# Two conditioning loads requested at another place, and the latents' copies put ahead of a split

## What is computed

```python
def modulated(x, g, mod, s):
    h = rmsnorm(x, g)
    return h * (1 + mod[:, s, 1][:, None]) + mod[:, s, 0][:, None]

for i in range(DEPTH):
    mod = silu(c) @ w_ada[i] + b_ada[i]             # 9 vectors of 1024 for each sequence
    x = x + 0.5 * g0 * swiglu(modulated(x, 0))
    x = x + g1 * (short_conv if i == 0 else mla)(modulated(x, 1))
    x = x + 0.5 * g2 * swiglu(modulated(x, 2))

# short_conv:  b, c, v = split(h @ w_in);  y = (b * conv(c * v)) @ w_out
# mla:         d = h @ w_in;  cq, ckv, kr = rmsnorm(d[:384]), rmsnorm(d[384:640]), rope(d[640:])
#              q = cq @ w_uq;  attention over ckv, kr and a paged cache;  @ w_o
```

## Time and profile before

| | us |
|---|---|
| median of 3 runs | 1253.67 |
| lowest and highest run | 1250.36, 1256.72 |
| the profiled execution | 1254.01 |
| its span | 1252.0 |

### The profile page before, as it was taken

How to read it: one execution, slowest core, us unless ns; L and a number is a source line. 1 busy time by engine, 2 the same in 40 slices (tenths; PEclk the granted TensorE clock), 3 DMA queues, 4 the chain that set the end, 5 groups by cost and what they waited for, 6 DMA issues and landing times.

```text
span 1252.0 us, 23786 instructions
## 1 busy us (share of the span) xinstructions
PE 1220.3 (97%) x9968; PEld 1142.7 (91%) x9968; DVE 674.0 (54%) x1021; ACT 523.9 (42%) x724; POOL 152.8 (12%) x144
## 2 busy tenths in 40 slices
PE   6999999999999999999999999998999999999997
PEld 5999999989999999999899999987776689999997
DVE  5545445466675444455544545456855466554453
ACT  4434343343335534433543433355633345454332
POOL 0000002300040000023000001210445040000031
PEclk9999999999999999999999999999999999999998
DMA  9877655468766774355677444575577563444442
GB/s 359 333 285 291 220 204 183 171 207 295 269 234 235 289 290 165 132 177 185 245 280 279 184 139 159 187 267 195 194 259 265 183 234 135 169 168 158 140 164 82
DMA packets 70617, 269.47 MB, mean 215 GB/s; under 512 B 5408, under 2 KB 5920, under 8 KB 56704
## 3 DMA queue, kind: packets, MB, share of 16 engines
q1 hardware_dynamic: 33888, 184.57, 40.5%
q10 hardware_dynamic: 29792, 59.09, 12.9%
q0 software_dynamic: 6848, 24.52, 5.9%
HBM read 266.55 MB, written 1.62 MB: 214 GB/s over the span
## 4 chain that ended last, share of the span: by engine, by line
PE 90%; DVE 4%; DMA 3%; ACT 2%; ACTq 1%; issue 1%; DVEq 0%; SPq 0%
PE bank L1473 24%; PE bank L1475 24%; PE bank L1474 24%; PE bank L1518 4%; PE bank L1858 3%; PE bank L1920 1%; PE bank L1872 1%; DVE w_lo L940 1%; ACT w_hi L677 1%; PE bank L1539 1%; ACTq L689 1%; PE bank L1540 1%; PE bank L1532 1%; PE bank L1646 1%; DMA stage<-in_w_uq 1%; DMA stage<-in_w_ci 1%
## 5 line engine op out<-in xcount | busy, mean ns | idle before, releaser
L940 DVE TENSOR_TENSOR w_lo<-stage,w_hi 128x2048 fp32r<-128x2048 f32 (+2 forms) x178 | 365.9, 2057 | 295.9 <-ACT w_hi L677 295.3
L1473 PE MATMUL bank<-h_hi,w_hi 128*128 128x288 f32 (+1 forms) x1576 | 467.8, 297 | 2.1 <-DVE w_lo L940 1.2
L1475 PE MATMUL bank<-h_hi,w_lo 128*128 128x288 f32 (+1 forms) x1576 | 465.0, 295 | 0.0
L1474 PE MATMUL bank<-h_lo,w_hi 128*128 128x288 f32 (+1 forms) x1576 | 464.4, 295 | 0.0
L677 ACT CAST w_hi<-stage 128x2048 fp32r<-128x2048 f32 (+2 forms) x178 | 296.7, 1669 | 251.4 <-PE bank L1475 175.6
L1473 PEld LDWEIGHTS bank<-h_hi,w_hi 128*128 128x128 f32 (+1 forms) x1576 | 295.5, 187 | 6.9 <-issue 3.3
L1475 PEld LDWEIGHTS bank<-h_hi,w_lo 128*128 128x128 f32 (+1 forms) x1576 | 295.5, 187 | 0.0
L1474 PEld LDWEIGHTS bank<-h_lo,w_hi 128*128 128x128 f32 (+1 forms) x1576 | 295.4, 187 | 0.0
L1475 PE MATMUL bank<-gu_hi,w_lo 128*128 128x288 f32 x768 | 227.6, 296 | 0.0
L1473 PE MATMUL bank<-gu_hi,w_hi 128*128 128x288 f32 x768 | 227.0, 296 | 0.0
L1474 PE MATMUL bank<-gu_lo,w_hi 128*128 128x288 f32 x768 | 224.0, 292 | 0.0
(11 more groups left out here) (263 smaller groups left out, 1049.7 us busy)
## 6 DMA issues: line engine op xcount, KB each, us to landing
stage<-in_w_gu SPq DMA_DIRECT2D x85, 1024.0 KB, 4.9
stage_ada<-in_w_ada ACTq DMA_DIRECT2D x53, 1024.0 KB, 9.3
stage<-in_w_down SPq DMA_DIRECT2D x64, 704.0 KB, 4.0
stage<-in_w_ci SPq DMA_DIRECT2D x16, 768.0 KB, 4.3
stage_ada<-in_w_ada SPq DMA_DIRECT2D x9, 1024.0 KB, 14.6
ada_early<-in_w_ada SPq DMA_DIRECT2D x4, 1024.0 KB, 16.6
stage<-in_w_co SPq DMA_DIRECT2D x4, 1024.0 KB, 6.9
stage<-in_w_wo SPq DMA_DIRECT2D x4, 1024.0 KB, 5.0
```

The costliest lines, as they stand in the source:

```text
L940: nc.vector.tensor_tensor(w_lo[part][:, 0:cols], stage[st_][:, 0:cols], w_hi[part][:, 0:cols], ALU.subtract).then_inc(lo_ready, 1)
L1473: nc.tensor.matmul(out, hi, x_hi, start=start, stop=False)
L1474: nc.tensor.matmul(out, hi, x_lo, start=False, stop=False)
L1475: return nc.tensor.matmul(out, lo, x_hi, start=False, stop=stop)
```

## The change

In the convolution's input product the four quarters of the second group are issued one in each of the four next steps with a unit (6 to 9), behind that step's split (`run`; `after` is told by `spaced` not to issue them). The latents' group is no longer issued by ScalarE: SyncE issues it ahead of its request of query unit 1, behind a wait for the last residual ahead of norm 4 (`x_ready`) and for the products of the group before (`ada_used`). In the last step of `mla_in` ScalarE copies the unit's tiles first and splits query unit 1 afterwards; in the two steps before the order stays.

```diff
--- before.py
+++ after.py
@@ -545,6 +545,11 @@
                 for st in steps(sp, seg, peel_first=seg.base == 0) if seg.n else ():
                     if st.u is None or isinstance(st.u, int) and st.u < OPEN_UNITS:
                         continue
+                    if st.kind == "uq" and st.place == 1:
+                        sp.wait_ge(x_ready, KT * MLA_BLOCK)
+                        sp.wait_ge(ada_used, LATENT + OPEN_MORE)
+                        for q in range(RING):
+                            sp.dma_start(by_run(ring_latent[q]), quarter(LATENT, q)).then_inc(ada_loaded[q], 16)
                     if isinstance(st.u, int) and st.u == OPEN_UNITS + 1:
                         sp.wait_ge(lo_ready, 1)
                     elif not isinstance(st.u, int) or st.u > OPEN_UNITS:
@@ -683,10 +688,10 @@
 
             SPACED = between_step(act, 1)
 
-            def load_ada(j, into=ring):
+            def load_ada(j):
 
                 for q in range(RING):
-                    act.dma_start(by_run(into[q]), quarter(j, q)).then_inc(ada_loaded[q], 16)
+                    act.dma_start(by_run(ring[q]), quarter(j, q)).then_inc(ada_loaded[q], 16)
 
             def root(n):
                 act.wait_ge(stats_ready, n + 1)
@@ -717,19 +722,18 @@
                     nc.scalar.activation(h_hi[:, kt, 0:TP], h_fp[:, kt, 0:TP], ACT.Identity,
                                          bias=mods[:, 3 * KT * n + kt, 0:1]).then_inc(h_hi_ready, 1)
                 if n == 1:
-                    after(SPACED)
+                    after(SPACED, spaced=True)
                 elif n and between_step(act, n):
                     after(between_step(act, n))
 
-            def after(st):
+            def after(st, spaced=False):
                 if st.kind == "ada":
                     act.wait_ge(ada_used, st.place + OPEN_MORE + 1)
                     act.wait_ge(asum_done, st.place + OPEN_MORE)
                     of = SUM_BANK.get(st.place, 6) if isinstance(st.place, int) else 6
                     nc.scalar.copy(ada_tok[:], bank[of][:, 0:2 * P]).then_inc(tok_copied, 1)
-                    if st is not SPACED and (not isinstance(st.place, int) or st.place < LATENT):
-                        load_ada(st.place + 1, ring_latent if isinstance(st.place, int) and st.place + 1 == LATENT
-                                 else ring)
+                    if not spaced and (not isinstance(st.place, int) or st.place + 1 < LATENT):
+                        load_ada(st.place + 1)
                 if st.kind == "gu":
                     m, n_m = st.tile, FT * st.unit.block + st.tile
                     act.wait_ge(unit_used, st.u + 1)
@@ -746,12 +750,16 @@
                     nc.scalar.copy(one(gu_hi, st.tile), conv_acc[:]).then_inc(y_hi_ready, 1)
 
             def run(name):
+                group, q = SPACED.place + 1, 0
                 for st in steps(act, SEG[name], split=True, peel_first=name == "ffn0_gu"):
                     split_ahead(st)
-                    if name == "conv_in" and st.u is not None and st.u - SEG[name].base in range(RING):
-                        q = st.u - SEG[name].base
-                        act.dma_start(by_run(ring[q]), quarter(SPACED.place + 1, q)).then_inc(ada_loaded[q], 16)
-                    after(st)
+                    if name == "conv_in" and st.u is not None and q < RING:
+                        act.dma_start(by_run(ring[q]), quarter(group, q)).then_inc(ada_loaded[q], 16)
+                        q += 1
+                    again = name == "conv_in" and st.kind == "ada" and st.place == SPACED.place + 1
+                    after(st, spaced=again)
+                    if again:
+                        group, q = st.place + 1, 0
 
             def open_h_hi(kt):
                 act.wait_ge(normed, kt + 1)
@@ -810,7 +818,9 @@
 
             norm(MLA_BLOCK)
             for st in steps(act, SEG["mla_in"], split=True):
-                split_ahead(st)
+                last = 2 * st.place + 2 > QT + RT
+                if not last:
+                    split_ahead(st)
                 act.wait_ge(unit_used, st.u + 1)
                 for b, t in zip(st.banks, range(st.tile, st.tile + 2)):
                     if t < QT + RT:
@@ -819,6 +829,9 @@
                     else:
                         nc.scalar.copy(kr_raw[0:ROPE], bank[b][0:ROPE, 0:T])
                         nc.scalar.copy(kr_raw[ROPE:P], bank[b][0:ROPE, 0:T]).then_inc(d_ready, 1)
+                if last:
+                    split_ahead(st)
+
             def latent_root(i, n, dst):
                 act.wait_ge(lat_stats, i + 1)
                 nc.scalar.activation(dst[:], bank[6 + i][:, 0:T], ACT.Sqrt, bias=eps[:, 0:1], scale=1.0 / n)\
```

## The result

| | before | after |
|---|---|---|
| median of the runs side by side (20 each), us | 1253.93 | 1256.57 |
| lowest and highest run, us | 1250.36, 1256.72 | 1254.32, 1259.36 |
| the profiled execution, its span, us | 1254.01, 1252.0 | 1256.49, 1254.9 |
| mean granted clock of the profiled execution | 0.997 | 0.993 |

The ratio is 1.0017, 95% interval 1.001 to 1.0024: **slower**, by about 2 us by the ratio and 2.6 by the medians, where 1.8 us faster was forecast. That is within 0.5%, but outside the range of 1249.0 to 1256.0.

A forecast was written before the change was run, and what follows sets the result against it. The prediction took TensorE as the bound, with only its gaps to win, 4.55 us or 0.36%. From 1254.01 us it took off 0.71 (convolution) and 1.09 (attention), giving 1252.2, range 1249.0 to 1256.0.

The forecast's parts named there:

- What bounds the kernel: Whole kernel: TensorE busy 1220.3 of 1252.0 us, so only its gaps can be won; the four total 4.55 us, 0.36%.
- The convolution: Convolution's input product: pacing the second group's quarters removes TensorE's gap; bounds 0 to 0.71 us gain, 0.71 taken.
- The latents' issues: Attention's input product: without ScalarE's issues unit 2 is split earlier, its 0.57 us gap goes, query unit 1 requested 4.0 us earlier.
- The landing: Attention: when query unit 1's load arrives behind the latents, between 848.0 and 850.3, against 849.97 today; 848.0 taken.
- The near end: Attention: query unit 1 lands at 848.0, by 7.37 MB at 384 GB/s; a gain of 1.09 us, taken.
- the far end: Attention: query unit 1 lands at 850.3, by 7.37 MB at 337 GB/s; a loss of 0.31 us.
- rival (a): Attention: latents ahead in the same ring delay query unit 1 to 848.7 to 851.7; 1253.5 us, chance 0.15.
- signs of being wrong: Query unit 1's cast waits for DMA and query product's gap exceeds 4 us; or units 12 and 13's casts stop TensorE.
- The reorder: Attention's last input step, copies before split: 1.52 us gap moves to the query product's start, nearly 3 us remaining there.
- (b): Attention: same ring lands query unit 1 from 850.7 on, losing more than the convolution wins; 1255.0 us, chance 0.11.
- (c): Convolution: its gap stays or moves because paced quarters delay units 12 and 13; 1252.9 us, chance 0.10.
- (d): Attention: unit 2's cast waited for something other than the issues, so the 0.57 us stay; 1252.8 us, chance 0.07.

The follow-up runs named there:

- experiment 1: Only the convolution's second group issued in four parts, against the kernel before; 1255.04 us, ratio 1.0002.
- experiment 8: Kernel before plus the convolution's part, latents still from ScalarE but two quarters behind the split in each of the first two input steps; 1253.67 us, ratio 0.9994.
- 9: Changed kernel without the reorder, query unit 1 requested by ScalarE instead of SyncE, latents early on SyncE; 1251.19 us, ratio 0.9969 to before.
- 5: Changed kernel without the reorder (split first, then copies), convolution and queue parts kept; 1254.29 us, ratio 0.9997 to before.
- 4: Changed kernel plus 14 filler matmuls in the gap ahead of the query product; 1253.82 us, ratio 0.9994 to before.
- 6: Kernel before with the reorder alone plus 12 filler matmuls in the gap ahead of the query product; 1253.75 us, ratio 0.9992 to before.
- experiment 3: Only the reorder (copies first, split second in the last input step), against the kernel before; 1255.83 us, ratio 1.0015.
- 2: Only the latents' group moved to SyncE's queue, copies still behind the split, against the kernel before; 1254.51 us, ratio 1.0003.

## Why the prediction was wrong

**What bounds the kernel: right.** Only gaps were to be won, under 0.5%. But the sentence was taken as a bound on gains alone; a gap can also cost more than its length, and no such loss was in the list of cases.

**The convolution: the edit works as said, its term was mis-sized.** 0.71 us was read from one execution, in which the bracket says 0.55. By the bracket five profiles with this stretch unchanged show 0.55, 0.24, 0.20, none and none (experiment 1), and neither the runs of the part alone nor the length of the stretch in ten profiles shows a gain that can be told from nothing. The bound "0 to 0.71" was right, the value should have been near its lower end.

**The latents' issues: right.** Unit 2's cast follows the copy at once, TensorE doesn't stop ahead of it, query unit 1 is requested 10.5 us behind the latents ("about 11"), and SyncE's new wait costs nothing.

**The landing: the term was mis-sized.** The near end, 848.0, was taken, the far end was 850.3. After's landing, 836.27 + 12.52 = 848.79, is 849.94 in the time of before (after is 1.15 us ahead there), just where it landed before (849.97). The rate held: it was 374 GB/s over the 21.6 us in question,

```profile
827.20:848.80 21.60, 21.60 (x165) 20.07 (x163) 8.81 (x14) 10.18 (x21) 3.20 (x7) 1.00 1.01 374
```

but these are 8.08 MB (374 × 21.6), not 7.37. Query unit 2, requested some 2 us behind query unit 1, flowed beside it and was not in the sum. With that 0.71 MB more at 384 GB/s the near end would have been 849.9. So rival (a), "one ring, later landing", is what happened in this term: 12.5 us in the common ring, 6.9 in a ring that doesn't hold the latents (experiment 8), 9.6 in ScalarE's with the latents early (9). Experiments 5 and 9 show it most closely, since only the queue of query unit 1 differs between them. This agrees with the rule quoted in the prediction from the Trainium skill ("DMA: Bandwidth & Descriptors", Queues, rings and completion order). The step behind the landing held: the query product follows the split by 856.50 − 848.81 = 7.69 us, where 7.85 was taken. Of the signs of being wrong, the cast waited for the DMA, but the gap stayed under 4 us. By rival (a) the time would be 1253.5; 3 us are still missing.

**The reorder: the step that failed.** The 1.52 us gap "moves to the query product's start", and "nearly 3 us of gap remain ahead of the query product". Both came true, 3.83 us with the late landing. But the gap was priced at its length, and of the work behind it the prediction said only that it "hangs on TensorE and moves with it": a loss of pace there was put at nothing, without a reason. In its place the profile shows the clock at 0.50 for 6 us and 2.49 us lost in the query product, and experiments 4 and 6, which fill only the idle time, take the loss away; experiment 3 makes it with the reorder alone. The kernel before has a granted clock of 1.00 in every stretch that was read around attention, with two gaps of 1.5 and 1.75 us and the latents' products between them. With these products between the gaps, the clock either held (before) or fell under a wait that was there anyway (experiments 2 and 5). The reorder took them away from there, and the prediction didn't ask what the merged gap does to the product behind it.

The Trainium skill ("TensorE: Matmul & The Clock Gate", HAM oscillation — how this bites in real kernels) describes this: where TensorE waits for a load between two bursts of matmuls, its clock goes back to half and the next burst starts slow. The trace agrees (3.83 us of wait, then 0.50). It prices the loss at half of the time spent at the low clock. With the 6 us of after's windows that is an estimate of 3 us, near the 2.49 measured.

The 1253.5 of rival (a) and the 2.49 make 1256.0, and the median was 1256.57. That this comes so near is partly luck: the 1253.5 holds 0.71 us of the convolution that the runs don't show, and the 1.8 us that after's profile lost behind 911 are not in it.

**The rivals.** (b), slower by the late ring alone, came out on the right side for the wrong reason: the landing was 0.8 us too early for it. (c) falls as a mechanism with the window at 310, though its price, no gain from the convolution, is what the runs show. (d) falls with the cast at 832.00.

**What stays open.** Half clock doesn't follow the long gap in every execution (experiment 3), and what decides it isn't shown. The slow stretches at 912 and in norm 2 are not explained. No run separates the 0.2 us of the convolution from scatter, and none the length of the merged gap from its place.

## What to carry to other kernels

Before gaps of TensorE are put together, ask what stands behind the new one: the same idle time in one piece ahead of a long run of matmuls can cost its length and then half speed on top, while in two pieces (1.52 and 1.75 us here) with work between it cost no more than its length. Behind waits of 2.0 to 2.3 us the clock already fell here: at next to no cost where TensorE would have waited again anyway (experiments 2 and 5), at 1.4 us where the query product stood there (8). Compare the mean granted clock over many runs, since one profile of a kernel can show the clock held. A load on the critical path does better in another queue than the bulk that is requested ahead of it, and what is requested behind it counts in its sum too.

## What was not expected of the hardware

The clock fell behind waits of 2.03 to 3.83 us at this place, in four of the five kernels that had them (in 3 the profiled execution held), and the stretches at half were some 3 to 7 us long. Over all kernels the order by mean clock nearly follows the order by longest gap. Loads of 0.79 MB that follow 4.19 MB in the same queue took 12.3 to 12.7 us each; in another queue than that bulk they took 6.9 to 9.6 (before, experiments 8 and 9).
